# w_out stage: eight additions onto the residual's first half by adding DMA transfers from GpSimd, not by VectorE

## The reference, cut to what matters

```
merged = sigmoid(g_sb) * (o_sb @ w_branch[:SB_W]) + sigmoid(g_ds) * (o_ds @ w_branch[SB_W:])
x = x + merged @ w_out                       # the stage of this change
h = rms_norm(x, ffn_norm_g)
u = causal_depthwise_conv(h @ w_up, conv_w, conv_b)
gate, val = jnp.split(u, 2, axis=-1)
x = x + (jax.nn.silu(gate) * val) @ w_down
```

## Time and profile before

| | |
|---|---|
| median of 3 runs | 1436.6 us (1436.59 to 1437.49) |
| span of the profiled execution | 1435.6 us |
| time of the profiled execution around its span | not recorded; the median is 1.0 us above the span |
| TensorE, VectorE, ScalarE, GpSimd busy | 1429.9, 1141.1, 843.4, 448.2 us |
| TensorE's granted clock | 1.00 of full speed |
| share of the chain that ended last | TensorE 98%, VectorE 1% |

### The profile page before, as it was taken

How to read it: one execution, slowest core, us unless ns; L and a number is a source line. 1 busy time by engine, 2 the same in 40 slices (tenths; PEclk the granted TensorE clock), 3 DMA queues, 4 the chain that set the end, 5 groups by cost and what they waited for, 6 DMA issues and landing times.

```text
span 1435.6 us, 23655 instructions
## 1 busy us (share of the span) xinstructions
PE 1429.9 (100%) x7578; PEld 1226.4 (85%) x7578; DVE 1141.1 (79%) x1534; ACT 843.4 (59%) x1182; POOL 448.2 (31%) x495
## 2 busy tenths in 40 slices
PE   9999999999999999999999999999999999999999
PEld 8888888888888888888888888888888888888887
DVE  6778998886556556889967778778778778999998
ACT  6646667566767766666665455454554545465553
POOL 2310000423232213650015455655556555200000
PEclk9999999999999999999999999999999999999999
DMA  8665665665555555567666666666666665676664
GB/s 250 189 191 175 204 198 184 196 185 173 154 173 148 174 166 184 182 218 243 184 185 179 189 192 188 180 192 190 197 187 181 188 192 189 193 232 206 203 207 147
DMA packets 121064, 272.24 MB, mean 190 GB/s; under 512 B 10689, under 2 KB 10977, under 8 KB 121009
## 3 DMA queue, kind: packets, MB, share of 16 engines
q1 hardware_dynamic: 119936, 268.99, 61.2%
q0 software_dynamic: 896, 2.42, 0.6%
q10 hardware_dynamic: 176, 0.14, 0.0%
HBM read 269.42 MB, written 2.10 MB: 189 GB/s over the span
## 4 chain that ended last, share of the span: by engine, by line
PE 98%; DVE 1%; DMA 0%; issue 0%; ACT 0%; DVEq 0%; ACTq 0%
PE bank L2100 97%; PE bank L2154 1%; DVE lo L1223 0%; DMA y<-in_x 0%; PE bank L2369 0%; PE bank L2410 0%; DVE y L1770 0%; PE bank L2237 0%; PE bank L2173 0%; DVE msum L1242 0%; ACT hi L720 0%; DVE msum L1251 0%; DVE msum L1248 0%; PE bank L2215 0%; DVE y L1815 0%
## 5 line engine op out<-in xcount | busy, mean ns | idle before, releaser
L1106 DVE TENSOR_TENSOR lo<-raw,hi 128x1024 fp32r<-128x1024 f32 (+1 forms) x342 | 444.9, 1306 | 166.3 <-ACT hi L637 165.3
L637 ACT ACTIVATE hi<-raw 128x1024 fp32r<-128x1024 f32 (+1 forms) x342 | 359.6, 1054 | 270.8 <-PE bank L2100 262.9
L2100 PE MATMUL bank<-h2T,hi 128*128 128x512 f32 x1408 | 483.3, 394 | 0.0
L2100 PE MATMUL bank<-h2T,lo 128*128 128x256 f32 x1408 | 376.8, 278 | 0.0
L2100 PEld LDWEIGHTS bank<-h2T,hi 128*128 128x128 f32 x1408 | 257.9, 188 | 53.5
L2100 PE MATMUL bank<-hT,hi 128*128 128x512 f32 (+1 forms) x784 | 272.8, 395 | 0.0
L2100 PEld LDWEIGHTS bank<-h2T,lo 128*128 128x128 f32 x1408 | 264.5, 188 | 7.8
L2100 PE MATMUL bank<-hT,lo 128*128 128x256 f32 (+1 forms) x784 | 212.6, 281 | 0.0
L2064 POOL TENSOR_TENSOR u<-u,rms_row 128x256 f32<-128x256 f32 x88 | 120.7, 1372 | 184.9 <-DVE u L1622 165.9
L2100 PE MATMUL bank<-hi,ffT 128*128 128x512 f32 x576 | 177.4, 389 | 0.0
L2100 PEld LDWEIGHTS bank<-hT,hi 128*128 128x128 f32 (+1 forms) x784 | 143.9, 187 | 29.3
(11 more groups left out here) (301 smaller groups left out, 2031.7 us busy)
## 6 DMA issues: line engine op xcount, KB each, us to landing
raw<-in_w_up SPq DMA_DIRECT2D x176, 512.0 KB, 3.8
raw<-in_w_in SPq DMA_DIRECT2D x160, 512.0 KB, 3.6
raw<-in_w_down SPq DMA_DIRECT2D x88, 512.0 KB, 4.5
raw<-in_w_branch SPq DMA_DIRECT2D x32, 512.0 KB, 3.6
raw<-in_w_out SPq DMA_DIRECT2D x24, 512.0 KB, 4.8
raw4h<-in_w_in SPq DMA_DIRECT2D x8, 512.0 KB, 3.7
raw5h<-in_w_in SPq DMA_DIRECT2D x8, 512.0 KB, 4.0
y<-in_x SPq DMA_DIRECT2D x4, 512.0 KB, 6.5
```

The lines of the kernel that those rows point to most:

```text
L637: act.activation(hi[s][:, 0:width], raw[s][:, 0:width], ACT.Copy)\
L1106: dve.tensor_tensor(lo[s][:, 0:width], raw[s][:, 0:width], hi[s][:, 0:width].bitcast(f32), ALU.subtract)\
L2100: return pe.matmul(o, l, r, start=start, stop=stop, skip_group_check=True)
```

## The change

VectorE's far adds of block 5 (`out_sums` with m = 0, n = 1 and 3) and its near adds (`out_near`) go. In their place GpSimd issues eight DMA transfers from `far_out` or `near_out` onto `y` with `accum_op=ALU.add`: the DMA engines read the destination, add the source and write. Two new semaphores count their landing: `far_added` and `near_added`. The waits that asked VectorE's count for them ask these now: ScalarE's far copy of block 6, `square` 0 to 3, TensorE's first transposes of y. The numbers in the other waits on `row_joined` are lower by eight. GpSimd's loads of x are in part moved: the two first far adds stand ahead of the loads of the second half, the other two between its third and fourth load, and the near adds behind all loads.

```diff
 # ScalarE: block_out, square
-                        if b > 2:
+                        if b == NB + 1:
+                            act.wait_ge(far_added, 16 * 4)
+                        elif b > 2:
...
-                act.wait_ge(row_joined, ROW_JOINS + 12 * (m + 1))
+                if m == 0:
+                    act.wait_ge(near_added, 16 * 4)
+                else:
+                    act.wait_ge(row_joined, ROW_JOINS + 16)
 # VectorE: out_sums
-                before = ROW_JOINS + 12 * m
+                before = ROW_JOINS + 4 * m
...
-                if n == 1:
+                if n == 1 and m == 1:
...
                 if n == 2:
+                    dve.wait_ge(row_joined, before + 2)
...
-                if n == 3:
+                if n == 3 and m == 1:
...
-            def out_near(o):
-
-                dve.wait_ge(near_copied, o + 1)
-                dve.wait_ge(row_joined, ROW_JOINS + 8)
-                out_add(0, o, near_out[o][:, :])
...
-                if c - OUT_AT[1] in (16, 17):
-                    for o in ((0, 1), (2, 3))[c - OUT_AT[1] - 16]:
-                        out_near(o)
 # GpSimd
-            for m, used in enumerate((C_OUT + 4, OUT_AT[1] + 2)):
-                if m:
-                    pool.wait_ge(row_joined, ROW_JOINS + 3)
-                for t in range(TH):
-                    for h in range(2):
-                        cols = slice(m * BLOCK + h * GRP, m * BLOCK + (h + 1) * GRP)
-                        pool.wait_ge(w_used, used + 3 * (2 * t + h))
-                        pool.dma_start(y[:, t, cols], x[0, t * P:(t + 1) * P, cols])\
-                            .then_inc(x_again, 16)
+            def load_x(m, o, used):
+
+                t, h = o // 2, o % 2
+                cols = slice(m * BLOCK + h * GRP, m * BLOCK + (h + 1) * GRP)
+                pool.wait_ge(w_used, used + 3 * o)
+                pool.dma_start(y[:, t, cols], x[0, t * P:(t + 1) * P, cols]).then_inc(x_again, 16)
+
+            def add_onto(o, term, done):
+
+                t, h = o // 2, o % 2
+                pool.dma_start(y[:, t, h * GRP:(h + 1) * GRP], term[:, :], accum_op=ALU.add)\
+                    .then_inc(done, 16)
+
+            for o in range(4):
+                load_x(0, o, C_OUT + 4)
+            one_, five, two, three = far_out[NB]
+            pool.wait_ge(x_again, 16 * 4)
+            pool.wait_ge(row_joined, ROW_JOINS + 2)
+            add_onto(0, one_, far_added)
+            add_onto(2, three, far_added)
+            for o in range(3):
+                load_x(1, o, OUT_AT[1] + 2)
+            pool.wait_ge(row_joined, ROW_JOINS + 4)
+            add_onto(1, two, far_added)
+            add_onto(3, five, far_added)
+            load_x(1, 3, OUT_AT[1] + 2)
+            pool.wait_ge(far_added, 16 * 4)
+            for o in range(4):
+                pool.wait_ge(near_copied, o + 1)
+                add_onto(o, near_out[o], near_added)
 # TensorE: rows_plain
-                        pe.wait_ge(row_joined, ROW_JOINS + 12)
+                        pe.wait_ge(near_added, 16 * 4)
```

More of the change, by code:

```diff
@@ L377, in hybrid_layer @@
         x_again = sem("x_again")
+        far_added = sem("far_added")
+        near_added = sem("near_added")
         const_set = sem("const_set")
@@ L1611, in _ @@
                 if c == C_UP + 2:
-                    dve.wait_ge(row_joined, ROW_JOINS + 20)
+                    dve.wait_ge(row_joined, ROW_JOINS + 12)
                     for o in range(4):
@@ L2475, in up_body @@
                         if first_pair and b == 0 and j < 6:
-                            pe.wait_ge(row_joined, ROW_JOINS + (22 if j == 0 else 24))
+                            pe.wait_ge(row_joined, ROW_JOINS + (14 if j == 0 else 16))
                             transposes(1, [4 + 2 * j, 5 + 2 * j], y)
```

## The result

The changed kernel takes 1440.96 us (median of 7 runs, 1439.62 to 1441.46) against 1436.6 us (7 runs, 1436.38 to 1437.49): ratio 1.0027, 95% interval 1.0018 to 1.0037. That is 4.4 us slower, inside the range that was given (up to 1441.0) by 0.04 us, but outside the 0.2% and the direction that were called likeliest.

A forecast was written before the change was run, and what follows sets the result against it. TensorE was taken as the bound, busy 1429.9 of 1435.6 us. Relief worth 0 and near adds landing at 696.05, before 697.65, gave no loss: 1436.6 us, range 1435.9 to 1441.0.

The forecast's parts named there:

- the 0.2%: Whole kernel: about 2.9 us, what a measurement can tell from no change; chance of staying within it 0.72.
- TensorE doesn't wait for VectorE, so the relief is worth 0: w_out stage: removing eight adds frees 4.8 us of VectorE, all ending in its idle time; TensorE gains nothing.
- Which wait is tight, and how much room it has: ScalarE's square, begun at 696.89 before, delays hi and lo of +19, then the bank adds TensorE needs: room 0.8 us.
- loss = T - 697.65: T is when the last near add lands; each microsecond of T past 697.65 us is one of the kernel.
- the value of L: Issue to landing of a 256 KB adding transfer: 5.8 us, with 3.5 and 8.2 as ends.
- The slow case in L: Far pair, then near adds: above L = 6.6 us each microsecond of L costs two.
- N = 688.45: GpSimd's near adds begin at 688.45 us, once the fourth load is issued and the far pair, started 682.65, has landed.
- doubled traffic: Near adds: each adding transfer loads the DMA engines like two loads; T = 699, loss 1.3, 1437.9 us; chance 0.30.
- its case of weights that keep their 164 GB/s: Doubled traffic with weights keeping 164 of 409 GB/s: near adds take 8.6 us, T = 700.7, loss 3.0.
- slow adds: Add slower than moving, or issue far above 0.6 us: L from 8.2 up, 1439.8 us at 8.2; chance 0.15.
- the rival's far end: Doubled traffic at the stage's own rate, 134 GB/s left: near adds take 15.7 us, T = 707.8, loss 10.2.
- The 1.0 us between span and time: Median 1436.6 us against the execution's span of 1435.6: 1.0 us taken as what lies around the span.

The follow-up runs named there:

- experiment 5: Against the kernel before: all eight additions left out, neither VectorE nor the DMA engines doing them; 1436.61 us against 1436.69, ratio 0.9998.
- Experiment 2: Against the changed kernel: ScalarE's four squares moved two chunks later, transfers unchanged; 1436.78 us, ratio 1.0002 to the kernel before.
- experiment 6: Against the changed kernel: two more adding transfers onto spare tiles, issued ahead of the near adds; 1446.01 us, 5.05 us more than the change.
- experiment 3: Against the changed kernel: the addition left out, so the eight transfers are plain copies; 1436.32 us, ratio 1.0000 to the kernel before.
- experiment 7: Separate program with only 256 KB copies and adding transfers, alone and beside paced weight loads; alone, the last of four lands 3.0 us later with addition.
- 4: Against the changed kernel: only the far adds stay adding transfers, VectorE does the near adds again; 1436.72 us, ratio 1.0002 to the kernel before.

## Why the prediction was wrong

- **TensorE doesn't wait for VectorE, so the relief is worth 0.** Right; experiment 5 shows it by itself.
- **Which wait is tight, and how much room it has.** Right: `square`, `hi` and `lo` of +19, then VectorE without idle time up to the bank adds. TensorE waits 1.62 us for the `lo` of +19, and the chain of the change goes through the bank adds. The wait of 0.85 us for the `lo` of the transposed tiles wasn't named; it lies on the same way and adds nothing to the sum, since the bank adds end last. The stated sum, loss = T - 697.65, gives for T = 699.87 + 1.0 (the shift of before's profile) a loss of 3.2 us; the profiled execution lost 3.2. Experiment 2 shows the path, and experiment 6, with the slow clock said there, the slope of one to one.
- **The step that failed** is the value of L: "I take 5.8 as the value, the upper end of the like loads, because the adds come four in a row." With it the last near add landed at T = 696.05 and the loss was 0. It measured 11.2 us for the last of four, which landed at T = 699.87 (700.9 on the clock of before's profile), and `square` began at 699.89. The term was mis-sized in two ways. The loads of x are copies (experiment 3: 6.3 us at this very place, near my 5.8), and an adding transfer keeps the engines busy 2.2 times as long as a copy (experiment 7). And one L was used for each of the four, while the four queue: 6.0 us for the first, 11.2 for the last.
- **The slow case in L was mis-stated too.** "Above it each microsecond of L costs two" assumed that the far pair lands as late as the near adds. The second add of the far pair landed 5.2 us after its issue, and near adds were issued from 687.04, 0.4 us ahead of the forecast (N = 688.45 less the 1 us). But a row of two can be late as well: the first far pair, issued at 663.1 and 663.7, took 7.4 and 9.4 us. There nobody waited for it.
- **The rival "doubled traffic" is what happened**, with T = 700.7 and loss 3.0 at its case of weights that keep their 164 GB/s (SyncE's queue moved 2.32 MB from 685 to 700, 155 GB/s); I gave it 0.30 and a middle of 1437.9 us. Its sign came too: landings that grow from the first near add to the fourth. The median of the runs lost 4.4, about 1.2 us more than the profiled one. A last add that lands near 701 would explain it, and in experiment 2 it did land 1.8 us later, but this isn't shown for those runs. That 1440.96 us falls inside the range is luck in part: its upper end was set for slow adds and the rival's far end as well. The Trainium skill ("Collectives: The Full Stack", section on the bandwidth ceiling) has it, of the ReduceScatter of a collective, that the addition costs no cycles, but needs two source reads and runs at half the rate. The trace agrees on the rate: 169 GB/s of destination against 372 while the engines are busy. Whether the reads are the cause no run here shows.
- **The 1.0 us between span and time** was wrongly read. Time less span is 1.9 us for the kernel before and 1.75 for the change; I had set the span of a run of 1437.49 us against the median. It changed no term, but it hid that the profile's stage lay 1 us late. The third theory, a loss outside the span, falls with it.
- **"Slow adds"** as a separate cause: experiment 7 speaks against it. GpSimd's issues stayed near 0.55 us apart, the far pair landed at 686.75 and not after 691, and ScalarE's far copy didn't wait. The idle times ahead of 702 and 714, which I had listed as its sign, belong to any late landing.

No version here beats the kernel before: the variants without loss (2, 3, 4, 5) are all at it, as they must be where TensorE has no idle time to give. Left open: how far the landing varies between runs of one kernel, of which one profile each was read.

## What to carry to other kernels

An adding DMA transfer was not priced by a load of the same size: counting its bytes twice came close here. Time the last one of a row, with the traffic beside it, not one by itself. Relieving an engine that the bounding engine never waits for buys nothing, so what replaces the work must be free to the microsecond. Before a wait is handed to a transfer, look at what is queued behind the waiting instruction: here moving four `square` by two chunks was worth 4.2 of the 4.4 us.

## What the runs showed of the hardware that was not expected

- Four adding transfers of 256 KB from SBUF to SBUF kept the DMA engines busy for 6.2 us, four copies for 2.8 us (169 and 372 GB/s of destination while busy), both from GpSimd's queue with nothing else moving.
- From 685 to 700 us, where four of them stand beside the weights and one load of x, the 16 DMA engines were at share 0.99; without them it was 0.55. In experiment 2 a weight load came so late that ScalarE stood 3.89 us for it.
- In 7.89 us without work TensorE's granted clock fell from 1.00 to 0.50, where it stayed until 711.50, 2.3 us after work began again (experiment 6); after the 1.62 us of the change it stayed at 1.00.
- In the trace GpSimd's instructions for adding transfers last 0.84 to 1.84 us each, but four begin within 1.7 us: they overlap, and the queue isn't held up as their length suggests.
